# A two-layer attention and DeltaNet trunk on one core: every engine's order of work inside a head rewritten, one slot per operation

## The reference

```python
p = (rmsnorm(x, norm_w) * (1.0 + sc) + sh) @ w_in
qa, ka, va, za, qkvb, zb, ab = split_in(p)
# group A: differential softmax attention
s = einsum('bhmqd,bhmkd->bhmqk', q, k) * (A_HEAD_DIM ** -0.5)
p = softmax(s); a = p[:, :, 0] - lam * p[:, :, 1]
y_a = rmsnorm(einsum('bhqk,bhkd->bhqd', a, v)) * (1 - lam_init) * silu(za)
# group B: gated DeltaNet in chunks, both directions; q, k, v through a 5-tap convolution and SiLU
sol = triangular_solve(m, rhs)          # a chunk's unit lower triangular matrix m
v_new = u_c - w_c @ state; state = state * exp(gl_c) + ke_c.T @ v_new
x = x + gt * (concatenate([y_a, y_b]) @ w_out)
```

## Time and profile before

| | |
|---|---|
| median of three runs | 2417.25 us (2413.26 to 2420.2) |
| span of the profiled execution, first to last instruction | 2410.9 us |
| the profiled execution's own device time | not recorded apart from its span |
| PE / PEld busy | 2206.6 us (92%) / 1762.7 us |
| DVE / ACT / POOL busy | 1424.9 us (59%) / 918.5 us (38%) / 143.5 us |
| mean granted TensorE clock | 0.959 |

### The profile page before, as it was taken

The page is one execution under the profiler, slowest core; times in us unless marked ns, Lnnn a source line. Parts: engine busy times, 40 slices in busy tenths (PEclk is TensorE's granted clock), DMA queues, the critical chain, the costliest instruction groups (busy, mean ns, idle before and its releaser), DMA issues. The chain is left out here.

```text
span 2410.9 us, 36951 instructions
## 1 busy us (share of the span) xinstructions
PE 2206.6 (92%) x13100; PEld 1762.7 (73%) x13100; DVE 1424.9 (59%) x2459; ACT 918.5 (38%) x1689; POOL 143.5 (6%) x183
## 2 busy tenths in 40 slices
PE   6789999999999999999999879798999989898887
PEld 3167777777778786877788658687777868787886
DVE  0333656656574747465664555657667575757675
ACT  3442434242423324242522364342424343352533
POOL 0000000000001000000100300000000001000002
PEclk8999999999999999999999989899999999999998
DMA  8974534353443535353645434434434343443664
GB/s 323 351 226 124 160 105 147 97 155 109 124 136 112 154 96 161 102 154 102 191 141 153 157 90 138 112 103 116 131 92 130 90 139 100 111 117 104 174 171 127
DMA packets 503952, 339.25 MB, mean 141 GB/s; under 512 B 63858, under 2 KB 465430, under 8 KB 503366
## 3 DMA queue, kind: packets, MB, share of 16 engines
q1 hardware_dynamic: 408854, 230.13, 33.7%
q10 hardware_dynamic: 94992, 108.09, 13.8%
q0 software_dynamic: 32, 0.07, 0.0%
HBM read 312.99 MB, written 25.23 MB: 140 GB/s over the span
## 5 line engine op out<-in xcount | busy, mean ns | idle before, releaser
L1827 PE MATMUL ps<-h_hi,w_hi 128*128 128x512 f32 (+1 forms) x2080 | 830.4, 399 | 17.1 <-DVE w_lo L1124 9.8
L1828 PE MATMUL ps<-h_lo,w_hi 128*128 128x512 f32 (+1 forms) x2080 | 774.5, 372 | 0.0
L1829 PE MATMUL ps<-h_hi,w_lo 128*128 128x512 f32 (+1 forms) x2080 | 773.9, 372 | 0.0
L1124 DVE TENSOR_TENSOR w_lo<-w_raw,w_hi 128x1024 fp32r<-128x1024 f32 (+1 forms) x300 | 365.5, 1219 | 273.1 <-ACT w_hi L671 233.4
L1827 PEld LDWEIGHTS ps<-h_hi,w_hi 128*128 128x128 f32 x2080 | 403.9, 194 | 131.4 <-issue 55.0
L671 ACT CAST w_hi<-w_raw 128x1024 fp32r<-128x1024 f32 (+1 forms) x300 | 311.3, 1038 | 377.4 <-PE ps L1829 164.7
L1829 PEld LDWEIGHTS ps<-h_hi,w_lo 128*128 128x128 f32 x2080 | 402.3, 193 | 70.7
L1828 PEld LDWEIGHTS ps<-h_lo,w_hi 128*128 128x128 f32 x2080 | 404.6, 195 | 51.3
L2115 PE MATMUL ps<-h_hi,w_hi 128*128 128x512 f32 (+1 forms) x448 | 158.0, 353 | 11.4 <-DVE h_lo L1124 7.2
L2117 PE MATMUL ps<-h_hi,w_lo 128*128 128x512 f32 (+1 forms) x448 | 152.6, 341 | 0.0
L2116 PE MATMUL ps<-h_lo,w_hi 128*128 128x512 f32 (+1 forms) x448 | 152.4, 340 | 0.0
(11 more groups left out here) (200 smaller groups left out, 2680.2 us busy)
## 6 DMA issues: line engine op xcount, KB each, us to landing
w_raw<-in_w_in SPq DMA_DIRECT2D x260, 512.0 KB, 4.1
ada_raw<-in_w_ada ACTq DMA_DIRECT2D x128, 512.0 KB, 4.6
w_raw<-in_w_out SPq DMA_DIRECT2D x36, 448.0 KB, 3.8
arena<-in_w_ada SPq DMA_DIRECT2D x27, 512.0 KB, 8.3
arena<-in_w_out SPq DMA_DIRECT2D x28, 448.0 KB, 4.0
w_raw<-in_w_ada SPq DMA_DIRECT2D x19, 512.0 KB, 8.5
ada_raw<-in_w_ada SPq DMA_DIRECT2D x18, 512.0 KB, 8.3
arena<-decay_rows ACTq DMA_DIRECT2D x16, 512.0 KB, 5.3
```

The source lines that it names most:

```text
L1124: return V.tensor_tensor(o, a, b, op)
L1827: mm(o, w_hi[:, s, k], h_hi[:, kt, t0:], start=kt == 0, stop=False)
L1828: before_last = mm(o, w_hi[:, s, k], h_lo[:, kt, t0:], start=False, stop=False)
L1829: last = mm(o, w_lo[:, s, k], h_hi[:, kt, t0:], start=False, stop=kt == KT - 1)
```

## The change

All the tables of slots (`SCORE`, `MIX`, `TURN_P`, `ADA_SLOT` and the others) are taken out. In their place stand three tables, `PE_AT`, `DVE_AT` and `ACT_AT`, each with one entry per operation and layer, with fractions, and the plan is written out in rising order (`for s in sorted(plan)`). The pieces of the projection, `split_hi` and `split_lo` keep their whole slots. No instruction is added or taken away, no buffer, size or semaphore changes, and SP's and POOL's programs are the same.

```diff
-        MIX = {0: (7, 17, 26, 35), 1: (7, 29)}
-        TURN_P = {0: (10, 19, 28, 37), 1: (10, 31)}
-        ADA_SLOT, ADA_EARLY = {0: (8, 12, 17, 20, 51, 55), 1: (10, 16)}, {0: 4, 1: 2}
+                "turn_p": (10.64, 18.56, 27.98, 35.29), "attend": (11.92, 20.91, 29.68, 37.4),
+                "gram": 6.57, "turn_p": (18.64, 32.67), "ada": (12.95, 22.54), "attend": (20.43, 33.2),
...
-                            put(MIX[layer][n], a_mix, n)
+                        for n in range(len(q_tiles[layer])):
+                            put(at["a_max"][n], a_max, n)
+                            put(at["a_mix"][n], a_mix, n)
                         for n in range(PIECES):
-                            put(SUBST[layer] + n, solve_blocks, n)
+                            put(at["solve_blocks"][n], solve_blocks, n)
...
-                    for s in range(SLOTS):
-                        if project and s % 4 == 2:
-                            split_lo(i, base + 2 + s // 4 + LEAD)
-                        for f, a in plan.get(s, ()):
+                    for s in sorted(plan):
+                        for f, a in plan[s]:
                             f(*a)
...
+                    def piece(s):
+                        if layer and isinstance(i, int) and i == 0 and s < 2 * SLOTS // UNITS:
+                            return
+                        k = s // 4
+                        t, half = k // 2, k % 2
+                        if s % 4 == 0:
+                            pe.wait_ge(w_split, i * UNITS + (base + 2 + k + 1))
+                            if half == 0:
+                                pe.wait_ge(evacuated, i * TILES + (layer * LAYER_TILES + 1 + t - 1))
+                        last = unit_piece(base + 2 + k, PJ + (1 + t) % 2, tokens(layer, t), half,
+                                          [2 * (s % 4), 2 * (s % 4) + 1])
+                        if s % 4 == 3:
+                            last.then_inc(w_used, 1)
```

More of the change, by code:

```diff
@@ L1012, in put @@
                         plan.setdefault(s, []).append((f, a))
-                    if not project:
+                    at = ACT_AT[layer]
+                    if project:
+                        for k in range(UNITS):
+                            put(4 * k + 1, split_hi, i, base + 2 + k + LEAD)
+                    else:
                         for n in range(4):
@@ L1031, in body @@
+                        put(at["q_grow"], q_grow)
+                        put(at["k_scale"], k_scale)
                         if project:
-                            put(LOAD_G, load_g, i, 0)
+                            put(at["load_g"], load_g, i, 0)
                         for j in range(4):
[L1034 to L1040, removed]
@@ L1041, in body @@
[L1041 to L1053 removed]
+                            put(at["v_new_copy"][j], v_new_copy, j)
@@ L1590, in body @@
+                        put(at["z_a"], z_silu, 0, 0)
+                        for k in range(1, ADA_IN[layer], 2):
+                            put(at["ada"][k // 2], ada, k)
                         if isinstance(i, int) and i == 0:
@@ new lines, in body @@
+                    at = PE_AT[layer]
+                    if project:
+                        for s in range(SLOTS):
+                            put(s, piece, s)
+                    if fill:
+                        put(at["turn_qk"], turn_qk)
+                        put(at["turn_va"], turn_va)
+                        put(at["turn_v"], turn_v)
+                        put(at["turn_back"], turn_back)
+                        put(at["gram"], gram)
+                        for d in range(2):
+                            put(at["times_m"][d], times_m, d, 0)
+                            put(at["times_inv"][d], times_inv, d, 0)
+                        put(at["corner_times_m"], corner_times_m)
+                        put(at["corner_times_inv"], corner_times_inv)
+                        for j in range(4):
+                            put(at["v_mul"][j], v_mul, j)
+                            if j < 3:
+                                put(at["s_mul"][j], s_mul, j)
+                                put(at["ks_mul"][j], ks_mul, j + 1)
+                        put(at["o_mul"], o_mul)
+                        put(at["turn_ob"], turn_ob)
+                        for n in range(len(q_tiles[layer])):
+                            put(at["score"][n], score, n)
+                            put(at["turn_p"][n], turn_p, n)
+                            put(at["attend"][n], attend, n)
+                        put(at["turn_oa"], turn_oa)
```

259 lines of the change are left out of this document (134 added, 125 removed).

## The result

The changed kernel takes **2297.8 us** (median of 4 runs, 2294.7 to 2303.2) against 2417.6: ratio 0.9516, 95% interval 0.9498 to 0.9534. That is 120 us less; the forecast was 98 less, 2319, with the range 2283 to 2372. The profiled execution has a span of 2296.1 us (device time 2299.2), so 114.8 less than the span of before.

A forecast was written before the change was run, and what follows sets the result against it. PE bounds the kernel (busy 2206.6 of 2410.9 us) through work, idle time and throttling. Gains of 35 (layer 0), 59 (layer 1) and 4 (edges) make 98: span 2312.9, plus 6.35 to the median, 2319 us; range 2283 to 2372.

The forecast's parts named there:

- Forecast 35 us: Layer 0's loop: turn_p's wait for a_mix and the clock's fall go, less new small waits; range 22 to 39.
- The order's sum: Layer 0, third softmax tile: durations added along the new order put the mix 1.6 us ahead of PE's turn_p.
- The 0.6 us per head for new waits: Layer 0: charge for chain ends, v_mul(1) and ks_mul(2), each waiting 0 to 0.5 us; seven heads.
- 13.4 - 9.9 = 3.5 us: Layer 1, second softmax tile: DVE's stretch less PE's work between score(1) and turn_p(1), the wait remaining per head.
- `turn_p`'s wait still 20 to 28 us: Sign of being right in layer 1's loop: turn_p would still wait this long in the changed profile.
- the 1.5 us per head of my upper bound: Layer 1, second modulation block: most PE would wait if its load kept 7.6 us; the sum would be 10 us smaller.
- Forecast 59: Layer 1's loop: gain in us, from 105 of waits and clock to 46; range 40 to 75.
- 4 forecast for the last head: Layer 1's last head: 4 us gained from turn_p(1)'s wait of 5.1 us, with its share of the clock.
- A part only: Rival, chance 0.22: two layer 0 chains late, layer 1's load keeps 1.5 us; gain 30 to 75, time 2342 to 2387.
- More: Rival, chance 0.08: DVE finishes layer 1's long stretch in 11 us; gain 120 to 150, time 2267 to 2297.
- The waits only move: Rival, chance 0.05: a buffer such as turn_p's PSUM tile causes the waits; time within 0.3% of 2417.
- Slower: Rival, chance 0.10: solved blocks' DRAM round trip ends later, each us costing 1 in each of 14 heads; example 2445.

The follow-up runs named there:

- the expectation above: Expectation for the changed kernel with layer 0's third a_mix put back about 3.1 us later; 2311 expected by its first theory, 2311.4 us measured.
- The runs with the buffer and with the mix moved: Changed kernel with a separate convolution buffer for tile BQ in layer 1, 2285.4 us; changed kernel with layer 1's second a_mix four solving pieces earlier, 2301.3 us.
- The last experiment: Changed kernel with layer 1's second modulation load issued again beside the blocks' load and a weight load, its product later: 2303.0 us.
- the run with buffer and mix: Changed kernel with tile BQ's own convolution buffer and, in layer 1, a_mix(1) ahead of the last solving pieces and the taps: 2296.3 us.
- the version it was made from: Changed kernel with BQ's own buffer, early a_mix(1), layer 1's chain behind the solved blocks later, layer 0's turn_back one piece later: 2284.3 us.
- the first run with the mix put back: Changed kernel with layer 0's third a_mix again behind two taps, a split_lo and the modulation's column, about 3.1 us later: 2311.4 us.

## Why the prediction was right, and where it was off

**Layer 0: right in cause and nearly in size.** Forecast 35 us, measured 39.3 in the loop. The order's sum said: mix done at 53.6, PE at `turn_p(2)` at 55.2, 1.6 us in hand. Counted from piece 0 like these, the trace has 54.3 and 55.6, 1.25 in hand (the 52.99 and 54.24 of the expectation above count from the first `turn_qk`, 1.35 us later). The 0.6 us per head for new waits came as 0.93, all of it at `turn_back`, which in layer 0 I had not singled out. The term that was too small is the clock: I took 15 of the 18 us that 0.98 stands for; PE's busy time fell by 20.7. That this one wait is the cause was shown: with 22.1 us of it again the loop is at 913.6. That the mix's move alone removed it was not: put back as far as it was, the mix brings back 1.6 of the 3.5 us per head, and by the times above the rest is the earlier start of the score's chain, which the prediction named too.

**Layer 1: the size of the remaining wait right, its place wrong.** I had kept "13.4 - 9.9 = 3.5 us" at `turn_p(1)`, and named "`turn_p`'s wait still 20 to 28 us" as the sign of being right. It is zero in the loop, and the 27.0 us stand elsewhere. The stretch from the end of `score(1)` to the end of the mix measured 13.25 us, and the wait 3.86 a head. But it stands one piece earlier, at piece 32, behind the copy that the last tap holds up. The step that failed is the list of who waits for DVE's long stretch: I followed the softmax chain through it, not the taps in it. That the number survived is luck: tap and mix end 1.3 us apart, and piece 32 happens to stand 1.36 us ahead of `turn_p(1)`. The runs with the buffer and with the mix moved settle this.

**The load.** I took its wait as zero, and it is: 25.4 us went. I had said "some 6.1 us after the issue's end" for PE; in this head of the changed kernel it was 5.6:

```profile
1877.01 0.94 ACTq L1027 DMA_DIRECT2D ada_raw<-in_w_ada  x2
...
1883.52 1.07 PE L1795 MATMUL ps<-ada_raw,c_T 128*32 128x256 f32 x16
```

The sum has two parts. One is the load's own time, with 1.5 MB of others issued around it before. The two halves' median to landing is 6.7 us before and 4.1 after:

```profile
ada_raw<-in_w_ada ACTq DMA_DIRECT2D x2, 512.0 KB, 6.7
```

```profile
ada_raw<-in_w_ada ACTq DMA_DIRECT2D x2, 512.0 KB, 4.1
```

The other is when PE comes: for the second half 6.0 us behind the issue's end now, 4.7 before. A landing as slow as before, 7.5 us, would still have cost the 1.5 us per head of my upper bound. The Trainium skill's rule of turns between queues ("DMA: Bandwidth & Descriptors", section "Queues, rings and completion order") agrees with this; what I had feared by it, that the load meets as much beside it as before, did not come about, since the block load had long gone. The last experiment shows the slow landing again when the loads are put together.

**Layer 1's total.** Forecast 59, measured 66.3. Idle time fell from 758.2 - 685.4 = 72.8 to 27.2, by 45.6, where I had 67.3 to 30. The difference is on both sides: 5.5 us of idle time before stood in none of the lines that I summed, and of the "0.85 us per head" of new waits at `turn_back` and hand-offs the view names none. Clock: I counted 22 of 38 as gained, PE's busy time fell by 20.7.

**The edges.** 4 forecast for the last head, 8.3 measured: its wait of 5.1 for the mix is 1.3 now, the output projection's waits for `ada_raw` and `h_lo` (L2115, now L2129) fell from 8.5 to 4.1, which I had set at nothing, and PE's busy time fell by 3.2; about 3 us of new small waits stand against this.

**From span to median.** I had added 6.35 us to the span. The changed kernel's median is 1.7 above its profiled span, and single executions have 2.1 to 3.1 between device time and span. The rest was, as it seems, that the profiled run of before was a quick one: its span of 2410.9 fits the lowest of the times, 2413.3, though its own time is not on record. That is some 5 of the 21 us by which the time lies under the forecast.

**The rivals.** A part only: the mechanism (chains in layer 0 late by 1 to 2 us, the load's 1.5) did not occur. More: its condition, `turn_p(1)` without a wait, came true by the letter, and the gain of 120 touches the lower end that I gave it; but not for its reason, DVE was not quicker (13.25 us, not 11). The waits only move: within the layer 1 head one did, from `turn_p(1)` to piece 32, 31.0 us against 27.0, and there a shared buffer does take part; but the 24.4 us of layer 0 and the load's 25.4 went with the order alone. Slower: not here, but the run with buffer and mix shows its wait, 3.1 us a head, as soon as the other waits go.

## What to carry to other kernels

When an operation is moved on an engine that another waits for, list every waiter of the stretch that it is moved through, not only the chain that one is following: the earliest pays, and removing it alone hands the time to the next (here piece 32, then `turn_p`, then `times_m`, then `turn_oa`, one behind the other in the same head). Where one operation moved, sums of durations along the order came within 0.3 us of three waits per head (1.9, 1.3 more and 3.1 expected, 1.6, 1.27 more and 3.2 measured). Where a whole chain moved they did not (none and 1 expected, 2.8 and 3.9 measured), and a move that was not summed for its consumers cost some 20 us against the version it was made from. What the clock takes behind a wait has to be measured as well: in layer 0 half the waiting cost less than half, but in layer 1 fourteen waits of 1.3 to 2.3 us (21.6 together) left the loop at 685.3 and seven of 3.2 (22.1 together) at 678.0, so many short waits are not always the cheaper ones.

## What the runs showed of the hardware that was not expected

In layer 0 of the first run with the mix put back the clock's answer to a wait was all or nothing: 1.00 behind waits of up to 1.8 us, 0.89 over the 16 us around waits of 1.9 and 2.3. It isn't a matter of one wait's length alone. In the run with buffer and mix two waits of 2.9 us together stood at the same place in two heads, and the granted clock over the 16 us there was 0.90 in one and 1.00 in the other (us, PE busy, granted clock, DMA share, GB/s):

```profile
1809.00:1825.00 16.00, 15.95 (x136) 0.90 0.42 107
...
1906.20:1922.20 16.00, 15.50 (x143) 1.00 0.38 107
```

Nor does a longer wait always cost more in layer 1's loop: with seven waits of 3.9 us at piece 32 PE was busy 664.7 us, with seven of 5.1 at the same place 657.5, with seven of 3.2 at `turn_p` 655.6. What decides between them stays open; no run here separates it.
